# Running sums of the stick-breaking heads by two rounded passes, the stick's two parts from ScalarE and VectorE, and the final norm's product on GpSimd

## The reference, cut to what matters

```python
def rmsnorm(x, g):
    y = x * lax.rsqrt(jnp.mean(x * x, axis=-1, keepdims=True) + EPS)
    return y * g
# end of the first block:  x = rmsnorm(h, final_norm_g)
# second block, 8 heads of 64:
z = jnp.einsum("bqhd,bkhd->bhqk", q, k) * scale
mask = s_idx < t_idx
log_beta = jax.nn.log_sigmoid(z)
log_one_minus = jnp.where(mask, jax.nn.log_sigmoid(-z), 0.0)
tail = lax.cumsum(log_one_minus, axis=3, reverse=True) - log_one_minus
weights = jnp.where(mask, jnp.exp(log_beta + tail), 0.0)
o = jnp.einsum("bhqk,bkhd->bqhd", weights, v)
# beside it: c = silu(layer_norm(conv31(glu_a * sigmoid(glu_b))))
x = x + concat([o, c]) @ w_out          # then norm, feed-forward, + x
```

## Time and profile before

| | us |
|---|---|
| median of 3 runs | 1236.39 (1236.01 to 1237.41) |
| profiled execution, whole | 1236.73 |
| its span in the trace | 1235.0 |
| PE busy | 1223.8 (99%) |
| DVE busy | 601.2 (49%) |
| ACT busy | 505.1 (41%) |
| POOL busy | 574.2 (46%) |

### The profile page before, as it was taken

One profiled execution on the slowest core, in us unless ns is written; L12 is line 12 of the kernel. 1 busy time (PEld: TensorE's weight loads), 2 busy tenths in 40 slices (PEclk: granted clock), 3 DMA queues, 4 the chain that ended last, 5 costly groups with the idle time before them and its releaser, 6 DMA issues.

```text
span 1235.0 us, 16489 instructions
## 1 busy us (share of the span) xinstructions
PE 1223.8 (99%) x5598; PEld 1004.6 (81%) x5598; DVE 601.2 (49%) x877; ACT 505.1 (41%) x674; POOL 574.2 (46%) x465
## 2 busy tenths in 40 slices
PE   9999999999999999999999999999999999999998
PEld 7888888888888888888888886768888888888887
DVE  6782435434653166414575879785334213321431
ACT  7532543343443144313473237666333223332331
POOL 5775553233445344453465441134454444444444
PEclk9999999999999999999999999999999999999999
DMA  8343332112333322232133321102232323223222
GB/s 298 124 145 126 118 103 69 51 69 68 102 102 104 102 85 93 94 119 84 64 124 104 101 86 51 35 18 85 71 104 98 117 88 102 86 85 120 81 76 81
DMA packets 34034, 118.41 MB, mean 96 GB/s; under 512 B 4032, under 2 KB 4160, under 8 KB 33856
## 3 DMA queue, kind: packets, MB, share of 16 engines
q1 hardware_dynamic: 33696, 117.49, 28.6%
q10 hardware_dynamic: 288, 0.24, 0.1%
HBM read 115.61 MB, written 2.10 MB: 95 GB/s over the span
## 4 chain that ended last, share of the span: by engine, by line
PE 95%; ACT 2%; DVE 1%; POOL 1%; issue 1%; DMA 0%; SPq 0%; POOLq 0%; ACTq 0%; DVEq 0%
PE ps L1240 29%; PE ps L1241 29%; PE ps L1242 29%; PE ps L1562 1%; PE ps L1407 1%; PE ps L1545 1%; PE ps L1298 1%; PE ps L1297 1%; PE ps L1296 1%; PE ps L1518 0%; PE ps L1306 0%; POOL w_lo L363 0%; PE ps L1603 0%; ACT slab L654 0%; POOL squares L431 0%
## 5 line engine op out<-in xcount | busy, mean ns | idle before, releaser
L363 POOL TENSOR_TENSOR w_lo<-w_raw,w_hi 128x512 fp32r<-128x512 f32 x430 | 555.3, 1315 | 621.8 <-ACT w_hi L464 355.7
L1240 PE MATMUL ps<-xg_hi,w_hi 128*128 128x512 f32 x960 | 375.7, 391 | 0.0
L1242 PE MATMUL ps<-xg_hi,w_lo 128*128 128x512 f32 x960 | 373.7, 389 | 0.0
L1241 PE MATMUL ps<-xg_lo,w_hi 128*128 128x512 f32 x960 | 373.6, 389 | 0.0
L1240 PE MATMUL ps<-y_hi,w_hi 128*128 128x512 f32 (+1 forms) x608 | 230.8, 380 | 0.0
L1241 PE MATMUL ps<-y_lo,w_hi 128*128 128x512 f32 (+1 forms) x608 | 229.8, 378 | 0.0
L1242 PE MATMUL ps<-y_hi,w_lo 128*128 128x512 f32 (+1 forms) x608 | 229.8, 378 | 0.0
L1240 PEld LDWEIGHTS ps<-xg_hi,w_hi 128*128 128x128 f32 x960 | 180.3, 188 | 37.8 <-issue 0.8
L1242 PEld LDWEIGHTS ps<-xg_hi,w_lo 128*128 128x128 f32 x960 | 180.2, 188 | 37.5
L1241 PEld LDWEIGHTS ps<-xg_lo,w_hi 128*128 128x128 f32 x960 | 180.3, 188 | 37.3 <-issue 0.5
L464 ACT ACTIVATE w_hi<-w_raw 128x1024 fp32r<-128x1024 f32 x124 | 130.5, 1053 | 126.0 <-PE ps L1242 126.0
(11 more groups left out here) (210 smaller groups left out, 1058.1 us busy)
## 6 DMA issues: line engine op xcount, KB each, us to landing
w_raw<-weights SPq DMA_DIRECT2D x199, 512.0 KB, 3.3
w_raw<-weights SPq DMA_DIRECT2D x16, 384.0 KB, 2.9
out_t<-h SPq DMA_DIRECT2D x8, 256.0 KB, 2.1
h<-x_t SPq DMA_DIRECT2D x3, 512.0 KB, 8.4
slab<-mem_t SPq DMA_DIRECT2D x2, 512.0 KB, 10.1
slab<-mats_in SPq DMA_DIRECT2D x1, 1024.0 KB, 7.3
w_raw<-weights SPq DMA_DIRECT2D x2, 256.0 KB, 3.9
h<-x_t SPq DMA_DIRECT2D x2, 256.0 KB, 4.4
```

What stands on the lines that cost most here:

```text
L363: nc.gpsimd.tensor_tensor(w_lo[:, s, half], w_raw[:, s, half], w_hi[:, s, half].bitcast(F32), ALU.subtract).then_inc(done, 1)
L1240: pe.matmul(out, w[0], x[0], start=first, stop=False)
L1241: pe.matmul(out, w[0], x[1], start=False, stop=False)
L1242: return pe.matmul(out, w[1], x[0], start=False, stop=last)
```

## The change

Three things are changed.

**The running sums.** `s_cumulate` no longer multiplies in float32. ACT makes a rounded float32r copy of each stick (`s_round(hd)`, a Copy over 1280 columns into the upper half of `y_hi` for even heads and `y_lo` for odd ones, raises `s_hi`), DVE makes the residue in place of the stick (`s_rest(hd)`, raises `s_lo`), and PE goes twice over the tiles, once with each part, with the triangle and the ones in float32r (their rounded copies are two more small DVE copies at the start). The three additions of `later_sums` are gone; each later tile is multiplied by the ones by itself, so a pass has 10 matmuls (512, 384, 256, 128, 384, 256, 128, 256, 128 and 128 columns).

**The masks.** The two masks of a head that lie in one PSUM bank are joined in one matmul of 2x128 columns: three for each head where there were four.

**The final norm's product.** DVE's `final_norm` is gone. POOL multiplies `h` by `final_bc` (two tiles behind each of the weight residues of blocks QK+8 to QK+11, eight in all), and the gain is multiplied in where DVE adds the residual: a scalar_tensor_tensor takes the place of a tensor_tensor.

The calls of `s_round` and `s_rest` are put into the written order, and ACT's `qk_squares_of(5)` comes ahead of `s_logs(3)`. The core of the diff:

```diff
+            pool.wait_ge(spread_copied, NORM_FINAL + 1)
+            for b in range(QK + 4, WOUT2):
+                weights_lo_next(b)
+                for m in (2 * (b - QK - 4), 2 * (b - QK - 4) + 1):
+                    nc.gpsimd.tensor_tensor(h[:, m, :], h[:, m, :], final_bc[:], ALU.mult).then_inc(final_done, 1)
...
+            def s_round(hd):
+                for n, c in enumerate(log_parts(hd), log_parts_ahead(hd)):
+                    act.wait_ge(s_stick, n + 1)
+                    if hd >= 2:
+                        act.wait_ge(s_cum, 2 * (hd - 1))
+                    nc.scalar.activation(stick_hi(hd)[:, c], stick_of(hd)[:, c], ACT.Copy).then_inc(s_hi, 1)
...
             s_logs(0)
             qk_squares_of(3)
+            s_round(0)
             s_logs(1)
             qk_squares_of(4)
+            s_round(1)
             qk_rstd_of(3)
...
+            s_round(4)
             s_logs(5)
             qk_squares_of(7)
+            s_round(5)
             s_weights(4)
             qk_rstd_of(7)
...
+                    if norm == NORM_TWO:
+                        nc.vector.scalar_tensor_tensor(out=new, in0=h[:, m, :], scalar=col("final_norm_g", m), in1=new,
+                                                       op0=ALU.mult, op1=ALU.add).then_inc(summed, 1)
...
+            def s_rest(hd):
+
+                t, hi, lo = stick_of(hd), stick_hi(hd), stick_lo(hd)
+                for n, c in enumerate(log_parts(hd), log_parts_ahead(hd)):
+                    dve.wait_ge(s_hi, n + 1)
+                    nc.vector.tensor_tensor(lo[:, c], t[:, c], hi[:, c].bitcast(F32), ALU.subtract).then_inc(s_lo, 1)
...
             s_softplus(1)
             qk_apply(3)
+            s_rest(1)
...
             s_softplus(4)
             pair_values_lo(1)
+            s_rest(4)
             qk_input(7)
             s_softplus(5)
             qk_apply(7)
+            s_rest(5)
             conv_taps(12)
...
+                    bank = 3 * (hd % 2)
+                    pe.matmul(ps[:, bank, 0:P], ident_r[:], far_below_r[:], start=False, stop=False, skip_group_check=True)
+                    pe.matmul(ps[:, bank + 1, :].rearrange("p (a t) -> p a t", t=P)[:, 0:4:3, :], ident_r[:],
+                              far_below_r[:].rearrange("p (a t) -> p a t", a=1).broadcast_to([P, 2, P]), start=False, stop=False,
+                              skip_group_check=True)
...
+                def sums_into(tile, stick):
+                    bank, at, n = TILES[tile]
+                    bank += 3 * (hd % 2)
+                    mm = pe.matmul(ps[:, bank, at:at + n], neg_tri_r[:], stick[:, AT[tile]:AT[tile] + n], start=False, stop=True,
+                                   skip_group_check=True)
+                    for later in range(tile + 1, ST):
+                        n = TILES[later][2]
+                        mm = pe.matmul(ps[:, bank, at + (later - tile) * P:at + (later - tile) * P + n], neg_ones_r[:],
+                                       stick[:, AT[later]:AT[later] + n], start=False, stop=True, skip_group_check=True)
+                    return mm
...
+                if hd != SPLIT_HEAD:
+                    ready(s_hi, 0)
+                    for group in tiles:
+                        for tile in group:
+                            sums_into(tile, stick_hi(hd))
+                    ready(s_lo, 0)
+                    for group in tiles:
+                        for tile in group:
+                            mm = sums_into(tile, stick_lo(hd))
+                        mm.then_inc(s_cum, 1)
```

More of the change, by code:

```diff
@@ L165, in build @@
         y_lo = sb("y_lo", [P, DT, SEQ], F32R)
-        slab = sb("slab", [P, 28 * SEQ])
+        with nc.sbuf_tensor("slab", [P, 28 * SEQ], F32) as slab:
+            pass
+        slab_r = sb("slab_r", [P, 28 * SEQ], F32R)
         memg_hi = y_hi[:, 4:8, :].rearrange("p a (b t) -> p (a b) t", b=2)
@@ L1216, in _ @@
             pair_values_lo(2)
+            s_rest(6)
             s_softplus(7)
+            s_rest(7)
             ln_centre()
-            final_norm(range(DT))
             assert not tap_order
@@ new lines, in pair_scores @@
+                    bank = 3 * (hd % 2)
[3 more added lines that the diff above has]
+                              skip_group_check=True)
+                    pe.matmul(ps[:, bank + 2, 0:P], ident_r[:], far_below_r[:], start=False, stop=False,
+                              skip_group_check=True).then_inc(s_z, 1)
@@ new lines, in s_cumulate, with ready @@
+            def s_cumulate(hd):
+                parts = log_parts(hd)
+                def ready(done, tile):
+                    c = slice(0, STICK) if len(parts) == 1 else (FIRST if tile == 0 else REST)
+                    pe.wait_ge(done, log_parts_ahead(hd) + parts.index(c) + 1)
+                def sums_into(tile, stick):
[8 more added lines that the diff above has]
+                    return mm
+                tiles = ((0,), (1, 2, 3)) if hd != SPLIT_HEAD else ((1, 2, 3), (0,))
+                if hd != SPLIT_HEAD:
[8 more added lines that the diff above has]
+                        mm.then_inc(s_cum, 1)
+                else:
+                    for group in tiles:
+                        ready(s_hi, group[0])
+                        for tile in group:
+                            sums_into(tile, stick_hi(hd))
+                        ready(s_lo, group[0])
+                        for tile in group:
+                            mm = sums_into(tile, stick_lo(hd))
+                        mm.then_inc(s_cum, 1)
```

88 lines of the change are left out of this document (28 added, 60 removed).

## The result

The changed kernel takes 1257.61 us (median of 4 runs, 1255.9 to 1258.01), the kernel before, on the same chip, 1236.82 (4 runs, 1236.01 to 1237.41). The ratio is 1.0166, 95% interval 1.0148 to 1.0184: 20.8 us slower. The forecast was 1253, with a range of 1243 to 1260. Two executions, one of the kernel before (2535.7 us) and one of a kernel with idle matmuls (3200.5 us), took over twice as long as all others and are left out of the ratios.

What follows compares the result with a forecast made beforehand. PE was taken as the bound, a queue of matmuls. Added waits of 22.6 us less 6.2 us of saved work gave 16.4; the walk's 16.2 us on 1236.73 gave 1252.9, stated as 1253, range 1243 to 1260.

Steps and rivals of the forecast that it cites:

- the walk: Row durations moved along the new written order from 744 us on: last channel sum 16.2 us late, 1249 to 1256; 54%.
- the clock rival: TensorE's clock halves behind PE's new long waits: 1.5 to 3 us for one, up to 6 or 7 for three; 1255 to 1260; 20%.
- the totals fit into idle time, what doesn't is the order: 10 us more on ACT and 12 on DVE fit, but ACT stands at each rounding until DVE makes the stick.
- the sums of heads 1, 3 and 5: Predicted sign: PE waits of 3 to 5 us there, put down to ACT's roundings or DVE's residues.
- Head 3's first pass on ACT: Predicted sign: it starts at about 780, ten us later than before, behind the squares of block 5.
- What PE saves: On PE, shorter sums save 5.2 us over 8 heads and joined masks 1.0; together 6.2 us of work.
- all stretches show a granted clock of 1.00: Trace before the change: TensorE at full 2.4 GHz everywhere, also in the stretch with a 1.6 us wait.
- landmarks: PE starts: scores of pairs 1, 2, 3 and the last channel sum, predicted 3, 6, 13 and 16 us late.
- Product on POOL: POOL's products hold up DVE's residues and taps; 12.4 us late without them, so they cost 3.8 us.
- Half covered: Rival: pairs 1 and 2 late by 6.1 us, taps' queue recovers in pairs 3 and 4; 1243 to 1248; 16%.
- everything covered: Rival: ACT and DVE finish roundings and residues during PE's blocks 5 to 7; PE saves 6.2 and 2.4 us; 1228; 6%.
- the slow form: Rival: float32r as slow as float32 in narrow shapes, 8.6 us a head, kernel at about 1290; 1%.

Runs made afterwards that it cites:

- the best order tried: Changed kernel, same instructions reordered: ACT passes over both heads of a pair before either rounding, DVE both sticks before residues; 1245.33 us. Also called the better or other order.
- the kernel with idle matmuls: Changed kernel plus matmuls with unused results in PE's long waits: first three places, 1255.19 us; then shorter waits too, 1251.92 us.
- the mixed order: The reordered kernel of 1245.33 us, with the changed kernel's order of steps put back at heads 6 and 7 only; 1245.54 us.
- a good part of the gain: Kernel before plus joined masks, with ACT's weight roundings of blocks QK+3 and QK+4 moved behind the weights of heads 0 and 1; 1233.75 us, 0.9976.
- the experiment with the weight blocks: Changed kernel with ACT's weight roundings of blocks QK+3 to QK+7 moved behind the weights of the same pair of heads; 1260.33 us, 1.0192.

## Why the prediction was right, and where it was not

The measured 1257.6 lies in the stated range, but not in the walk's own 1249 to 1256, which had 54%. It lies in the clock rival's 1255 to 1260, which had 20%.

**Direction and mechanism: right.** The step "the totals fit into idle time, what doesn't is the order" held: the same instructions in another order are 12 us faster. The other 8.8 us stay with the two-pass form in the best order tried. PE's waits were named at the sums of heads 1, 3 and 5, for roundings or residues. They measured 3.3 and 1.1, 4.6, and 3.5 us, where the walk said 3.5 and 2.5, 4.8, and 3.8. Head 3's first pass on ACT was put at 780.1 and came at 781.97; 1.6 of the 1.9 us lie ahead of it already, at the scores of pair 1. That heads 2 and 4 would wait less than 1 us held too. At heads 6 and 7 the walk had 3.7 and 1.7 us; they were 1.8 and 2.4. At the last values the walk had 2.9 us of waiting, and there is none.

**What PE saves: right.** A pass without a wait takes 1.4 us (786.04 to 787.4), as worked out, from another mix: behind a matmul of 128 columns with the ones the next starts after 0.06 us, where 0.12 was taken, and those with the triangle take a little more (0.28 us for 512 columns where 0.22 was taken). The masks gave 0.7 us of 1.0.

**The clock: in the wrong place in the sum.** It was a rival at 20%, of 1.5 to 3 us for one wait. All the waits of 3 us and more had the low clock behind them, and one of 2.43 us had it a pass later. The step that failed is "all stretches show a granted clock of 1.00", taken as the likelier outcome for waits of 3 to 5 us. The row behind it has a wait of 1.6 us only; it said nothing of twice that length. The forecast of 1253 is what the kernel with idle matmuls measured (1251.92), and its landmarks (2.9, 6.4, 12.4, 14.9) follow the walk's (3.1, 6.1, 12.9, 16.2). The mis-sized term is thus the clock: 0 in the sum, about 5 us by these runs. The slow work read alone is more: head 1 and the sum of squares behind it some 3.3 us, head 3 2.7, head 5 and the scores 2.2, head 7 1.1 and the values behind it 0.7, 10 in all. A part lies beside waits: head 1's residue ended a wait of 1.07 us behind a slow pass and one of 2.31 behind a fast one. The rival had "up to 6 or 7"; as a net cost that was right.

The terms of the sum say the same. The walk had 22.6 us of waiting more than before, 6.2 of work saved and no slow work, 16.4 late. Measured are 15.8 us of waiting more (19.5 against 3.7), 10 of slow work and, if the 6.2 are right, 19.6 late, against the 19.2 of the landmark. The waiting alone is thus 6.8 us short of the walk's, because slow sums fill time in which PE would else have waited: with idle matmuls (14.9 late, plus 6.2) it comes to 21.1.

**Product on POOL: wrong.** The walk gave it 3.8 us; it costs some 1 us here, not told from nothing, and none in the kernel before. The single holdings were as expected (2.04 us for a residue instead of 1.49, 8.71 for twelve taps instead of 7.69). What failed is the step from a held tap to a late end: the walk let every late stick through to PE and set nothing against it. The prediction says that the eight products leave DVE "at a place where nobody waits". But the 0.72 us wait for POOL's channel sum stands there, and with the product on POOL it is gone (changed kernel, and the product alone) or down to 0.2 us. Without the product the walk was 12.4 late; with 1 us for it that makes 13.4, against the 14.9 with idle matmuls, so its other terms were too small by up to 1.5 us together. Which, isn't settled: the kernel with idle matmuls and without the product was not run.

**Half covered, everything covered, the slow form: did not come.** The landmarks kept on growing through heads 4 and 5, by 5.2 us, and through heads 6 and 7, by 3.5.

What stays open: whether a two-pass form can win at all. The best order tried leaves it 8.8 us behind, with waits of 3.96 us at head 0 and 5.74 at head 6; there the mixed order showed that swapping the steps moves the wait and not the end. How much of these 8.8 us is the clock is open too, since the better order was not run with idle matmuls.

## What to carry to other kernels

Before adding a step on an idle engine between two others, write down the queue of that engine at that place: what counts is the round from PE through ACT and DVE and back, not the sum of idle time. Price a new wait on PE twice, once for itself and once for the slow work behind it. And when work moves on one engine, look at who follows it: here POOL's residues follow ACT's roundings, and beside POOL the additions, taps and residues of DVE, all with both inputs in SBUF, slowed down. The same coupling gave a good part of the gain (two additions from 1.9 and 2.7 us to 0.5) and spoiled the experiment with the weight blocks.

## What the runs showed of the hardware

**The clock.** In these traces the granted clock fell to 0.50 only in or shortly behind a wait of PE, but the length of the wait tells neither whether nor when.

- It fell while PE still stood, in waits of 3.32, 4.62 and 3.50 us (changed kernel), 3.96 and 5.74 (the other order) and 2.23 (weight blocks later).
- It fell with PE back at work, 0.7 us after the end of a wait of 3.62 (weight blocks later), 0.6 after one of 2.31 (idle matmuls), 0.9 after one of 1.94 (masks and product) and 1.9 after one of 2.43 (changed kernel, head 7).
- The same wait of 2.43 us had no fall behind it in the two kernels with the product on DVE. Waits of 1.6 to 1.9 us mostly had none, but one of 1.82 had in both kernels with idle matmuls.
- Shorter waits add up or don't: it fell behind 1.30 and 1.18 us with short work in between, and in the kernel in which DVE rounds it stayed at 1.00 from 750 to 765 us, with four waits of 0.9 to 1.3 us.

At 0.50 a matmul of 512 columns starts the next 0.53 us later instead of 0.28 in the same place of a pass, and the float32 one of the sum of squares takes 1.81 us instead of 0.95. The Trainium skill (TensorE: Matmul & The Clock Gate, on what is happening) has the clock gated by recent activity and halved when idle; these rows agree, and add that the fall can come when PE is at work again.

**Matmuls of 128 columns.** In float32r the next matmul starts 0.06 us after one of 128 columns with the ones, and 0.11 after one with the triangle (787.26 to 787.32, 785.92 to 786.04). The rows don't say why: every matmul has its own weight load in the trace (5606 of each), and the 0.06 are there too where the matmul ahead had the other weights.

**DVE beside POOL.** A residue of 1280 columns took 1.49 us alone and 1.56 to 2.04 beside POOL (up to 2.48 in the kernel with the other order), and the stick's maximum, which has one input in PSUM, 1.49 either way (786.01 beside POOL, 805.63 alone); POOL itself took 3.8 instead of 2.5 us for two operations of 512 columns when DVE was at residues and taps. The Trainium skill (SBUF — State Buffer, on SBUF's two sides) has the loser of the shared port pair blocked for the whole instruction; that both engines slow down in turn agrees with it.
